# The next head's softplus beside this turn's value products, sums over key blocks on VectorE, and the first scores inside the projection: a hybrid decoder layer pair on one core

## The reference, cut to what matters

```python
def _stick_breaking(q, k, v, mask, bias):
    z = jnp.einsum('bthd,bshd->bhts', q, k) * (DH_B ** -0.5) + bias[None, :, None, None]
    log_stay = jnp.where(mask, jax.nn.log_sigmoid(-z), 0.0)
    after = lax.cumsum(log_stay, axis=3, reverse=True)
    after = jnp.concatenate([after[..., 1:], jnp.zeros_like(after[..., :1])], axis=-1)
    w = jnp.where(mask, jnp.exp(jax.nn.log_sigmoid(z) + after), 0.0)
    return jnp.einsum('bhts,bshd->bthd', w, v)
```

## Time and profile before

| what | value |
|---|---|
| median of 3 runs | 1841.87 us (1837.36 to 1848.1) |
| the profiled execution | 1839.33 us, of which the span of its instructions is 1837.7 us |
| mean granted TensorE clock | 0.941 |
| PE busy | 1661.6 us, 90% of the span |
| DVE, ACT, POOL busy | 889.3, 591.6, 91.0 us |
| transfers | 195.11 MB, mean 106 GB/s |
| key pages, value pages | 128 of 256 KB each |

### The profile page before, as it was taken

How to read it: one execution, slowest core, us unless ns; L and a number is a source line. 1 busy time by engine, 2 the same in 40 slices (tenths; PEclk the granted TensorE clock), 3 DMA queues, 4 the chain that set the end, 5 groups by cost and what they waited for, 6 DMA issues and landing times.

```text
span 1837.7 us, 31417 instructions
## 1 busy us (share of the span) xinstructions
PE 1661.6 (90%) x12398; PEld 1475.3 (80%) x12398; DVE 889.3 (48%) x1510; ACT 591.6 (32%) x937; POOL 91.0 (5%) x168
## 2 busy tenths in 40 slices
PE   6899986786887999999999988998879999999996
PEld 6899982333333999999999978996669999999996
DVE  4545443335343384444444564675545644444445
ACT  4222222243232462222222543324225422222224
POOL 0000001112212000000000000000000000000000
PEclk9899997788888999999999989998889999999998
DMA  4221137678764222222222221123202122222221
GB/s 173 103 69 70 58 116 262 198 224 261 230 195 142 94 71 87 72 91 91 91 91 70 77 79 61 47 94 115 91 35 78 61 93 91 91 79 81 84 76 51
DMA packets 50519, 195.11 MB, mean 106 GB/s; under 512 B 7325, under 2 KB 9534, under 8 KB 36610
## 3 DMA queue, kind: packets, MB, share of 16 engines
q1 hardware_dynamic: 35938, 139.49, 22.1%
q0 software_dynamic: 14496, 54.41, 8.7%
HBM read 182.19 MB, written 11.68 MB: 105 GB/s over the span
## 4 chain that ended last, share of the span: by engine, by line
PE 83%; DVE 8%; ACT 3%; issue 3%; SPq 2%; DMA 1%; DVEq 0%; POOLq 0%; POOL 0%; ACTq 0%
PE ps L298 21%; PE ps L300 21%; PE ps L299 20%; PE ps L1265 2%; PE ps L1293 2%; PE ps L1438 1%; PE ps L1441 1%; ACT whi L290 1%; PE ps L1474 1%; DVE wlo L294 1%; SPq L1242 1%; PE ps L1396 1%; PE ps L1897 1%; PE ps L1444 1%; DVE sp L1429 1%
## 5 line engine op out<-in xcount | busy, mean ns | idle before, releaser
L298 PE MATMUL ps<-xhi,whi 128*128 128x280 f32 x2112 | 627.2, 297 | 30.2 <-DVE wlo L294 17.5
L300 PE MATMUL ps<-xhi,wlo 128*128 128x280 f32 x2112 | 620.7, 294 | 0.0
L299 PE MATMUL ps<-xlo,whi 128*128 128x280 f32 x2112 | 620.0, 294 | 0.2 <-issue 0.2
L298 PEld LDWEIGHTS ps<-xhi,whi 128*128 128x128 f32 x2112 | 403.2, 191 | 36.4 <-DVE wlo L294 19.4
L299 PEld LDWEIGHTS ps<-xlo,whi 128*128 128x128 f32 x2112 | 402.7, 191 | 1.0 <-issue 0.5
L300 PEld LDWEIGHTS ps<-xhi,wlo 128*128 128x128 f32 x2112 | 402.6, 191 | 0.0
L294 DVE TENSOR_TENSOR wlo<-raw,whi 128x2048 fp32r<-128x2048 f32 x98 | 224.6, 2292 | 212.8 <-ACT whi L290 212.3
L290 ACT ACTIVATE whi<-raw 128x2048 fp32r<-128x2048 f32 x98 | 187.3, 1912 | 421.0 <-PE ps L300 420.2
L298 PE MATMUL ps<-dhi,whi 128*128 128x280 f32 x1024 | 300.5, 293 | 5.1 <-DVE wlo L294 4.6
L300 PE MATMUL ps<-dhi,wlo 128*128 128x280 f32 x1024 | 300.2, 293 | 0.0
L299 PE MATMUL ps<-dlo,whi 128*128 128x280 f32 x1024 | 299.2, 292 | 0.0
(11 more groups left out here) (378 smaller groups left out, 1586.3 us busy)
## 6 DMA issues: line engine op xcount, KB each, us to landing
raw<-in_weights_dram SPq DMA_DIRECT2D x98, 1024.0 KB, 4.8
kbuf<-in_k_cache_dram SPq DMA_DIRECT2D x128, 256.0 KB, 3.1
vbuf<-in_v_cache_dram POOLq DMA_DIRECT2D x128, 256.0 KB, 3.5
s0b<-in_gla_in_dram POOLq DMA_DIRECT2D x4, 1024.0 KB, 5.4
out_dram<-s0b POOLq DMA_DIRECT2D x4, 1024.0 KB, 4.1
hT<-in_x_dram SPq DMA_DIRECT2D x2, 1120.0 KB, 8.3
out_dram<-pj POOLq DMA_DIRECT2D x2, 1120.0 KB, 7.0
hT<-in_x_dram POOLq DMA_DIRECT2D x2, 1120.0 KB, 7.5
```

The costliest lines, as they stand in the source:

```text
L298: pe.matmul(out, whi[:, par, t, :], hi, start=first, stop=False)
L299: pe.matmul(out, whi[:, par, t, :], lo, start=False, stop=False)
L300: return pe.matmul(out, wlo[:, par, t, :], hi, start=False, stop=last)
```

## The change

It moves work between engines and places, all inside the attention and the last projection pair.

- **Inclusive sums.** The weight is now exp(z minus the sum of softplus from this key on, this key included), so `psp_dve` makes only the softplus and no log-sigmoid. A new constant `incl` (one where row >= column) takes the place of `after` for the blocks' own sums.
- **Later blocks added first.** DVE adds the softplus of later key blocks into `T_` (inside `lz`), and PE takes one product of ones with each sum in place of one with each block.
- **Mask before the exponential.** `pmask_dve` adds a large negative number (`negs`) before `pexp_act` in place of multiplying after it. The weights now lie in `sp`, so `psoft_act` no longer waits for the value products; `psp_dve` does.
- **Order.** The next head's prompt scores come ahead of its page scores; the collection of a turn's page outputs (`own_out_pe`, `pout_dve`, `page_out`) comes one turn later; ACT makes the next head's softplus (`psoft_act`) right after its scores, and the meta rows' part after the page scores.
- **Beside the projection.** The last projection pair has `ahead_pe`, `ahead_act`, `ahead_dve` beside its groups: the decode tokens' own scores, the first head's scores, softplus and values.
- **Buffers and queues.** `kbuf` and `vbuf` lie elsewhere in memory. SP loads three of the first four key groups once the last mLSTM head is done, the fourth after the projection. POOL loads the values ahead of storing the new keys and values (`kv_out`), and reloads `hT` when all key pages have been read. Buffers per stream stay at one turn.

```diff
+        def ahead_pe(pe, n):
+            if n == 0:
+                new_scores_pe(pe)
+            elif n == 1:
+                pz_pe(pe, 0, 0, 4)
+            elif n == 3:
+                new_suffix_pe(pe)
+            elif n == 5:
+                values_pe(pe, 0, 0)
...
         def psoft_act(act, i, u):
-            if u:
-                act.wait_ge(S["a_v"], i * 2 + u)
...
         def psp_dve(dve, i, j):
+            if j:
+                dve.wait_ge(S["a_v"], i * 2 + j)
             for n, (r, c) in enumerate(FULL):
                 dve.wait_ge(S["a_l"], i * 4 + (2 * j + n + 1))
                 own.link(dve.scalar_tensor_tensor(sp[r, c], z[r, c], 0.0, lz[r, c], ALU.max, ALU.add))
-                own.link(dve.scalar_tensor_tensor(z[r, c], z[r, c], 0.0, lz[r, c], ALU.min, ALU.subtract))
             diag_mask(dve, sp, sp[0:N_META, METAQ]).then_inc(S["a_sp"], 1)
+            dve.wait_ge(S["a_sp"], i * 2 + (j + 1))
+            blk = lambda k, q, n=1: sp[:, KOFF[k] + P * (q - k):KOFF[k] + P * (q - k + n)]
+            own.link(dve.tensor_tensor(T_[0], blk(2, 3), blk(3, 3), ALU.add))
+            dve.tensor_tensor(T_[1][:, P:2 * P], blk(1, 3), T_[0], ALU.add)
+            own.link(dve.tensor_tensor(T_[1][:, 0:P], blk(1, 2), blk(2, 2), ALU.add))
+            dve.tensor_tensor(T_[2][:, 0:P], blk(0, 1), blk(1, 1), ALU.add)
+            dve.tensor_tensor(T_[2][:, P:3 * P], blk(0, 2, 2), T_[1], ALU.add).then_inc(S["a_T"], 1)
...
         def load_keys(sp_):
+            sp_.wait_ge(S["m_mix"], H_A)
+            sp_.wait_ge(S["mout"], 64)
+            for g in range(3):
+                load_k(sp_, 0, 0, g)
+            sp_.wait_ge(S["done"], DONE["out0"])
+            load_k(sp_, 0, 0, 3)
             for g in range(4):
-                load_k(sp_, 0, 0, g)
+                load_k(sp_, 0, 1, g)
...
         def attn_pe(pe):
+            new_turn_pe(pe)
+            suffixes_pe(pe, 0, 0)
+            new_values_pe(pe)
+            pz_pe(pe, 0, 1)
+            qk_pe(pe, 0, 0)
+            pv_prompt_pe(pe, 0, 0)
+            tr_pe(pe, 0, 0)
+            suffix_pe(pe, 0, 0)
+            qk_pe(pe, 0, 1)
+            tr_pe(pe, 0, 1)
+            pv_pe(pe, 0, 0)
             def step(i, u, last):
                 suffixes_pe(pe, i, u)
+                own_out_pe(pe, i, u - 1)
                 suffix_pe(pe, i, u)
                 if not last:
+                    pz_pe(pe, i, u + 1)
+                if u == 2:
+                    values_pe(pe, i, u)
+                if not last:
                     qk_pe(pe, i, u + 1)
-                    pz_pe(pe, i, u + 1)
                 pv_prompt_pe(pe, i, u)
                 if not last:
                     tr_pe(pe, i, u + 1)
                 pv_pe(pe, i, u)
-                own_out_pe(pe, i, u)
-                if u == 1 and not last:
-                    values_pe(pe, i, u + 1)
...
+            pool.wait_ge(S["cld"], 16 * N_CONST)
+            load_values(pool)
             pool.wait_ge(S["ev"], EV["even"] + 56)
             for b in range(2):
                 pool.dma_start(kv_out[:, 4 * b:4 * b + 4, :], pj[:, KBB + 4 * b:KBB + 4 * b + 4, :]).then_inc(S["out"], 16)
-            pool.wait_ge(S["cld"], 16 * N_CONST)
-            load_values(pool)
+            pool.wait_ge(S["k_used"], 36)
             for h in range(2):
                 pool.dma_start(hT[:, :, COLS[h]], x[:, :, COLS[h]]).then_inc(S["xr"], 16)
```

More of the change, by code:

```diff
@@ L216, in build @@
         ROWN = 4 * DEC_B
[L217 to L221, removed]
+        o_K2 = o_M + 18 * ROW
+        kbuf = [at(f"kbuf{g}", (o_hT, o_hT + GB, o_K2, o_hi + GB)[g], [P, PG, 4, P]) for g in range(4)]
+        vbuf = [at(f"vbuf{g}", o_M + g * GB, [P, PG, 4 * P]) for g in range(4)]
+        assert 4 * GB <= 16 * ROW and 2 * GB <= KB * ROW
+        o = o_K2 + GB
         qbd = at("qbd", o, [P, 4, DEC_B, 8]); o += 1024
@@ L1489, in turns @@
                     own.start(i, own_steps)
-                for u in range(2):
+                for u in (1, 2):
                     step(i, u, False)
@@ new lines, in ahead_first_dve, with ahead_dve @@
+        def ahead_first_dve(dve):
+            dve.wait_ge(S["rout"], 32)
+            dve.wait_ge(S["ev"], EV["even"] + 48)
+            new_queries_dve(dve)
+            own.link(dve.memset(qz[:, :, :], 0.0))
+            pair_in_dve(dve, 0, 0, values=False)
+        def ahead_dve(dve, n):
+            if n == 0:
+                new_scores_dve(dve)
+                dve.tensor_tensor(incl[:, :], ones, strict, ALU.subtract)
+                dve.tensor_scalar(negs[:, :], strict, 1.0, -NEG, ALU.subtract, ALU.mult)
+            elif n == 1:
+                new_soft_dve(dve)
+            elif n == 2:
+                dve.memset(sg[:, :, 0:1], 0.0)
+                own.link(dve.memset(smk[:, :, :], 1.0))
+                own.link(dve.memset(smk[:, :, 0:1], 0.0))
+            elif n == 3:
+                new_sub_dve(dve)
+            elif n == 4:
+                dve.wait_ge(S["ev"], EV["even"] + 53)
+                first_values_dve(dve)
+                new_mask_dve(dve)
+            elif n == 5:
+                psp_dve(dve, 0, 0)
+            elif n == 6:
+                values_dve(dve, 0, 0)
@@ L1522, in step @@
                 pv_pe(pe, i, u)
[L1523 to L1532 removed]
+            later_turns(pe, step)
+            own_out_pe(pe, 3, 1)
+        def attn_act(act):
+            pexp_act(act, 0, 0)
+            act.wait_ge(S["mout"], 80)
+            pz_act(act, 0, 1)
+            page_z_act(act, 0, 0)
+            page_act(act, 0, 0)
+            psoft_act(act, 0, 1)
+            page_exp(act, 0, 0)
+            psoft_meta_act(act, 0, 1)
+            page_z_act(act, 0, 1)
+            page_act(act, 0, 1)
             def step(i, u, last):
```

278 lines of the change are left out of this document (159 added, 119 removed).

## The result

| | before | after |
|---|---|---|
| median | 1842.11 us (4 runs, 1837.36 to 1848.1) | 1777.44 us (4 runs, 1774.57 to 1781.94) |
| ratio | | 0.965, 95% interval 0.9612 to 0.9687 |
| profiled execution, its span | 1839.33, 1837.7 us | 1774.83, 1773.2 us |
| first, last `pv_pe` end | 341.39, 593.38 us | 325.62, 529.59 us |
| mean turn between them | 36.0 us | 29.14 us |

What follows compares the result with a forecast made beforehand. After the change, refilling the single value buffer bounds a turn at 29.2 us, where PE and DVE waiting on each other took 36.0. Savings 15.4 + 47.6 - 1 = 62 us off 1839.33 give 1777 us, range 1755 to 1803.

Steps and rivals of the forecast that it cites:

- head: Up to the end of the first `pv_pe`: about 326 us where it was 341.39, 15.4 us saved.
- tail: After the last `pv_pe`: 3.5 us as before, with 1 us (0 to 5) lost to the later `hT` reload.
- the value stream's terms: Refill of the single value buffer in a turn: 27.2 us, plus 2.0 for slow products, 29.2 us.
- rival 2: Turns: waits cost full half rate, or key and value pages collide longer; about 32.3 us, total 1800; chance 0.17.
- rival 1: Turns: the clock stays at 2.4 GHz through the waits; 27.2 us per turn, total 1763 us; chance 0.17.
- The key stream: Refill of the single key buffer in a turn: 24.8 us (24.2 to 26.6).
- a sign of being wrong: PE's waits in the changed kernel: ending with `kbuf` would mean that key loading is the bound.
- PE's own work: PE's sums, products and collection in a turn: 23.3 us, near 1 us more in each second turn.
- the ring: Chain through ACT and DVE in a turn, from the softplus on: 23.2 us, with handing over 23.5.
- the four limits: A turn lasts as long as the longest: PE work 23.3, ACT and DVE chain 23.5, key refill 24.8, value refill 27.2.
- Rival 4: Value pages issued more slowly: at 2.2 us intervals a turn is 41.5 us, total about 1863; chance 0.03.
- rival 3: Turns: the DVE wait closes elsewhere and they stay at 36 us; only the start gains, about 1825 us; chance 0.03.

Runs made afterwards that it cites:

- numbers first for the values alone: Changed kernel with page numbers read into registers ahead on the value queue (GpSimd) only, key queue looking each up as before: 1800.4 us, ratio 0.9809.
- the two undone parts: Changed kernel with the page output collection put back: 1803.73 us; changed kernel with the ahead steps after the last projection pair instead of beside it: 1791.02 us.
- numbers first on both queues: Changed kernel with both queues reading a turn's sixteen page numbers into registers before waiting for the buffer: 1739.76 us, ratio 0.9463.
- the filler: Changed kernel with two 512-column products that nobody reads ahead of `pv_pe` in each turn: 1778.16 us, ratio 0.9685.

## Why the prediction was right, and what in it was wrong

The time (1777 against 1777.44) and the steps of the sum held: head 15.4 against 15.8, turns 47.6 against 48.0, tail -1 against +0.7 (`hT` was not late). The bound was named rightly: in the middle turns PE waits for `vbuf` (1.0 to 3.2 us; I had 2 to 4), and shortening the issues moved the time by 37 us. But **the value stream's terms were mis-sized and made up for each other**, which is luck:

| term, us | predicted | one middle turn |
|---|---|---|
| `pv_pe` to the first issue | 1.15 | 0.47 |
| sixteen issues | 18.78 | 18.77 |
| last landing | 3.6 | 5.3 |
| products at 2.4 GHz (behind the wait: 26 records) | 3.7 | 3.62 |
| lost to 1.2 GHz | 2.0 | 1.7 |
| sum | 29.2 | 29.86 |

- The mean of 29.14 against 29.2 is in part luck too: the seven turns last 30.27, 29.76, 28.17, 29.86, 27.94, 26.76 and 31.21 us. In the last POOL stood still for 3.23 us between its first and second issue, as it did in that turn of the kernel before (564.82), where 36 us hid it; the prediction gave all turns the same stream, and no run shows the cause.
- The first issue came 1.3 us after `pv_pe` in the first two turns, as before, and 0.37 to 0.47 after it in the others. Why, no run shows.
- The landing. I took the median of a turn in which the value pages ended alone. In the shorter turn the next keys begin beside the last values. That is rival 2's collision in part; in full (33.9 us in the turn shown, 1800 us) it came only in another kernel, the run with numbers first for the values alone.
- The clock. `pv_pe` did not begin at 1.2 GHz: in the turn shown the granted clock was 2.4 GHz up to 439.2, most of 1 us behind the wait, 1.2 GHz from 439.6 to 442.4, and 2.4 again from 442.8. The next turn lost nothing to it, as PE's timeline shows, and lasted 27.94 us (443.68 to 471.62):

```profile
468.00 3.62 PE L1323 MATMUL ps<-vbuf,lg 128*32 128x512 f32 x26 [3.16 <-DMA vbuf<-in_v_cache_dram]
```

Over the seven turns the loss was nearer 1 us than 2, and in some of them rival 1 held.
- The key stream. I had 24.8 us and called it hidden. In the first two turns PE waited 3.89 and 2.46 us for keys (for values 0 and 1.03), which the prediction names as a sign of being wrong: there the value stream was not the bound, or not alone. From one `qk_pe`'s end (320.61) to the next (348.48) it took 27.9 us: the sixteen pages were all there 22.5 us after the first end (21.2 in my sum), and the products took 5.32 behind the wait (3.57).
- PE's own work (23.3) was right within a microsecond, the ring (23.5) was not longer, and DVE's sums were ready before `pv_pe` ended. That VectorE's additions would not matter follows from the four limits: the 2.3 us that they save PE lay under a stream of 27. Two slips in the working change nothing: the ones take five products of 128 columns and not four (3088 counts five), and the ring's terms from 12.2 on add up to 23.0, not 23.2.
- By the fit in the Trainium skill's page "DMA: Bandwidth & Descriptors" (section "Anatomy of one DMA — SWDGE (gpsimd) path"), a page of 256 KB takes an estimated 2.6 us. In the last turn, where no keys are loaded, a page landed in 2.8 to 3.7 us (median 3.1); with both queues at work in 2.9 to 5.3 in the turn shown, and in up to 11.3 with numbers first for the values alone. So the estimate for one transfer alone did not tell the landing time of two streams.
- Rival 4 (values issued more slowly beside DVE) did not come: the idle time ahead of an issue stayed 0.68 to 0.78 in the turn shown. That the change does nothing (rival 3) is excluded by the two undone parts, 26 and 13.6 us.

What of the rest belongs to the inclusive sums without a log-sigmoid, and what to the mask ahead of the exponential, wasn't tried apart.

## What to carry to other kernels

When a wait on an engine is taken out, work out at once the refill time of every single buffer in the loop, issue by issue; the shortest turn is the longest of these, and work saved elsewhere (the sums) shows only after that one is shortened too. Read the landing time from a stretch in which the same transfers meet as will meet in the new turn, not from the old one. A page table lookup between two transfers costs half of their interval; reading the numbers ahead was worth 37 us here and nothing in the kernel before, and doing it on the value queue alone cost 23 and on the key queue alone gained nothing.

## What the runs showed of the hardware

- A faster queue slowed the other one down: with values issued every 0.6 us and keys every 1.2, keys landed in up to 11.0 us and the kernel lost 23 us. While both had work waiting (398 to 412 us), the two queues moved nearly equal numbers of packets (1032 and 1006) but packets of unequal size (3.28 and 1.82 KB). That agrees with the Trainium skill's page "DMA: Bandwidth & Descriptors", section "Queues, rings and completion order": each engine takes turns between its queue rows by packets. Why POOL's packets are larger, and whether the profile's packets are the page's, no run here shows.
- With numbers first on both queues the 16 DMA engines carried 343 to 355 GB/s over whole turns, at a share of 0.95 to 0.97.
- The same 26 value products after an idle 3.16 us took 3.62 us in one turn, after 2.92 us 5.32 in another (mean granted clock over these products: all and 0.67 of 2.4 GHz), and with the filler 5.32 after 2.12: how long PE had idled alone does not tell which level follows.
